# In layer two's expert loop, the preceding block's down products go in front of the last quarter of the up products, and the addition to the tokens goes behind it

## What is computed

```
out = 0
for e in range(16):
    g_, u_ = split(t @ w_gu[e])                        # w_gu[e] is 1024 x 1024
    out += gates[:, e] * ((silu(g_) * u_) @ w_dn[e])   # w_dn[e] is 512 x 1024
h = layer_norm(alpha * h + g2 * out)
```

## Time and profile before

| | |
|---|---|
| time, median of 3 runs | 1627.43 us (1623.88 to 1629.74) |
| profiled execution: its own time | 1631.9 us |
| profiled execution: its span, first to last instruction | 1630.1 us |
| PE busy over the span | 1527.2 us (94%) |
| DVE, ACT, POOL busy over the span | 871.2, 371.1, 271.4 us (53%, 23%, 17%) |
| mean granted TensorE clock | 0.979 of full speed |
| HBM read | 356.66 MB |

### The profile page before, as it was taken

How to read it: one execution, slowest core, us unless ns; L and a number is a source line. 1 busy time by engine, 2 the same in 40 slices (tenths; PEclk the granted TensorE clock), 3 DMA queues, 4 the chain that set the end, 5 groups by cost and what they waited for, 6 DMA issues and landing times.

```text
span 1630.1 us, 31680 instructions
## 1 busy us (share of the span) xinstructions
PE 1527.2 (94%) x13300; PEld 973.5 (60%) x13300; DVE 871.2 (53%) x1553; ACT 371.1 (23%) x893; POOL 271.4 (17%) x303
## 2 busy tenths in 40 slices
PE   6999999899999999898999886999999998999984
PEld 3454576564444468665666455757688887565642
DVE  3159946576777743652336437494552126554445
ACT  1100047541000010422222122003651002121211
POOL 0300000101112300042334230000000001543321
PEclk9999999999999999999999997999999999999998
DMA  9633220105857961999669968443125467999993
GB/s 319 195 104 94 78 68 27 51 28 182 274 154 247 326 222 63 357 414 385 240 261 407 414 271 303 145 120 98 48 61 189 143 220 285 396 415 415 414 416 115
DMA packets 147455, 365.23 MB, mean 224 GB/s; under 512 B 11265, under 2 KB 90729, under 8 KB 130419
## 3 DMA queue, kind: packets, MB, share of 16 engines
q1 hardware_dynamic: 125536, 296.86, 49.0%
q0 software_dynamic: 19328, 60.62, 11.1%
q10 hardware_dynamic: 2451, 5.73, 1.1%
HBM read 356.66 MB, written 10.62 MB: 225 GB/s over the span
## 4 chain that ended last, share of the span: by engine, by line
PE 66%; DVE 5%; DMA 5%; ACT 2%; SPq 1%; issue 1%; DVEq 0%; ACTq 0%; POOLq 0%
PE psum L1166 64%; DMA yab<-in_moe_w_gu 3%; DMA arena<-in_moe_w_gu 1%; PE psum L1703 1%; SPq L931 1%; DVE ring L2772 1%; PE psum L1450 0%; DMA convT<-us,x_row 0%; DVE st L2197 0%; DVE H L2794 0%; DMA yab<-ys 0%; DVE st L2198 0%; PE psum L1272 0%; DVE H L2210 0%; ACT uT L1870 0%
## 5 line engine op out<-in xcount | busy, mean ns | idle before, releaser
L1166 PE MATMUL psum<-uT,ring 128*128 128x512 f32 (+1 forms) x1440 | 494.7, 501 | 5.1 <-ACT uT L1870 2.1
L1166 PEld LDWEIGHTS psum<-uT,ring 128*128 128x128 f32 x1440 | 272.9, 191 | 215.1 <-issue 196.8
L1166 PE MATMUL psum<-ring,mo_tok 128*32 128x256 f32 x4992 | 313.0, 385 | 21.9 <-DVE ring L2772 21.7
L1166 PEld LDWEIGHTS psum<-ring,mo_tok 128*32 128x32 f32 x4992 | 157.4, 111 | 127.2 <-DVE ring L2772 28.5
L1166 PE MATMUL psum<-ring,v_tok 128*32 128x256 f32 x2496 | 152.1, 385 | 0.5 <-ACT v_tok L2119 0.5
L2350 DVE SCALAR_TENSOR_TENSOR convT<-upad_extra,cwT,convT 128x512 f32<-128x512 f32 (+1 forms) x240 | 132.4, 614 | 2.1
L1166 PEld LDWEIGHTS psum<-ring,v_tok 128*32 128x32 f32 x2496 | 82.4, 112 | 56.3 <-issue 3.8
L1166 PE MATMUL psum<-ring,uT 128*128 128x256 f32 (+1 forms) x576 | 113.1, 357 | 0.0
L1166 PEld LDWEIGHTS psum<-ring,uT 128*128 128x128 f32 x576 | 99.3, 190 | 15.5 <-issue 4.2
L1166 PE MATMUL psum<-yab,ring 128*128 128x512 f32 (+1 forms) x256 | 85.2, 486 | 0.0
L1166 PE MATMUL psum<-qkT_mqk 32*128 32x256 f32 (+5 forms) x752 | 81.3, 410 | 2.8 <-DVE qkT_mqk L2733 0.9
(11 more groups left out here) (364 smaller groups left out, 1633.0 us busy)
## 6 DMA issues: line engine op xcount, KB each, us to landing
ring<-in_w_in SPq DMA_DIRECT2D x104, 512.0 KB, 4.8
uT<-in_moe_w_gu SPq DMA_DIRECT2D x22, 1024.0 KB
yab<-in_moe_w_gu SPq DMA_DIRECT2D x21, 1024.0 KB
arena<-in_moe_w_gu SPq DMA_DIRECT2D x21, 1024.0 KB
ring<-in_w_mod SPq DMA_DIRECT2D x32, 512.0 KB, 9.7
mv_tok<-in_w_mod POOLq DMA_DIRECT2D x32, 512.0 KB, 5.2
convT<-in_w_mod POOLq DMA_DIRECT2D x32, 512.0 KB, 5.6
qkT_mqk<-in_moe_w_gu SPq DMA_DIRECT2D x14, 1024.0 KB, 16.4
```

The source lines that it names most:

```text
L1166: return nc.tensor.matmul(dst, lhsT, rhs, start=start, stop=stop)
```

## The change

In the second layer only, `down(b - 1)` moves from the end of iteration b to the place behind `up(b, (4, 5))`, and `add_to_tokens(b - 2)` moves from there behind `up(b, (6, 7))`, to the end of the iteration. The first layer's order stays.

```diff
                     if b < nb:
                         up(b, (4, 5), loads)
+                    if l and b:
+                        down(b - 1, loads_before)
+                    if b < nb:
                         for p, i in quad_halves(l, b):
                             quad_transposes(p, i)
+                        up(b, (6, 7), loads)
                     if l and b >= 2:
                         add_to_tokens(b - 2)
-                    if b < nb:
-                        up(b, (6, 7), loads)
-                    if b:
+                    if l == 0 and b:
                         down(b - 1, loads_before)
```

## The result

| | before | after |
|---|---|---|
| median of the runs, us | 1628.59 (1623.88 to 1629.74, 4 runs) | 1646.52 (1645.72 to 1648.4, 4 runs) |
| ratio, with its 95% interval | | 1.0118 (1.0094 to 1.0142) |
| profiled execution, own time, us | 1631.9 | 1648.4 (span 1646.6) |

The change makes the kernel slower by 1.2%, some 18 us by the medians. The forecast was 42.3 us. The sign, the place and the engine that TensorE now waits for came out as forecast; the size is the second rival's, not the first's.

What follows compares the result with a forecast made beforehand. TensorE was taken to bound the stretch of experts with several blocks; 25.3 + 6 + 1.5 + 8 + 1.5 = 42.3 us on the median 1627.4 gave 1669 us, 2.6% slower. Range 1643 to 1684, likeliest 1660 to 1682.

Steps and rivals of the forecast that it cites:

- rival 2: GpSimd slips in between two copies: eleven iterations lose 1.2 us each, total 15, with clock drops 20; 1642 to 1648; chance 0.26.
- the first's: The forecast itself: both waits, half clock in none to all of eleven iterations; 1660 to 1679, or 1682; chance 0.57.
- U + 0.28: GpSimd's matrix, held by the late addition, starts 0.28 us after an iteration's start U and ends at U + 1.50.
- Down's cover by pair 2: Pair 2 alone covers down's wait for ScalarE's hidden-row copy; no loss taken, 3 us as upper bound.
- The releaser named by the chain: At the loop's end the chain of waits names a transfer landing at 1593.66; the prediction called that misleading.
- One shuts out the other for whole instructions: VectorE copies and GpSimd instructions block each other fully; GpSimd gets nothing done between two copies in a row.
- eleven iterations under two copies: Iterations 3 to 25 where a new expert's copies start: hidden rows end behind both copies, 2.3 us lost each, 25.3 us.
- twelve others: Remaining iterations from 3 to 25: transposes wait for hidden rows behind the late matrix, 0.5 us each, 6 us.
- eleven iterations with quad transposes: Quad transposes move by the same steps and cost the same, so no loss.
- the end, from iteration 26: Iteration 26 to the last addition: down's gain is lost again to GpSimd; 53.05 us against 51.6, 1.5 us more.
- half clock: Stalls of 2.3 us may halve TensorE's clock: 8 us for the eleven, 1.5 us for the single-block stretch.

Runs made afterwards that it cites:

- the halved transfers: Kernel before, with the last two experts' weight transfers cut to half their bytes: 1625.9 us, ratio 0.9998; the same cut with a third matrix buffer in the new order: 1618.83 us.
- the third buffer: Kernel after, with room for three matrices, so block b's matrix waits for the addition of block b-3: 1625.68 us, ratio 0.9997 to before.
- down alone: Against the kernel before, only down moves forward, and the addition stays ahead of pair 3's products: 1629.04 us, ratio 1.0021.
- the addition alone: Against the kernel before, only the addition moves to the iteration's end; down keeps its place behind pair 3: 1666.75 us, ratio 1.0247.
- one-input hidden rows: Kernel after, with layer two's hidden rows made by a TENSOR_SCALAR, silu factor left out: 1669.76 us, ratio 1.0256 to before.

## Why the prediction was right in kind and wrong in size

**Right.** TensorE bounds the stretch, so a wait there costs its full length. The matrix stands behind the late addition and starts at U + 0.28 (measured 0.28). GpSimd's hidden rows are the releaser in eleven long and twelve short waits. The sign that the prediction gave for rival 2, eleven stalls near 1.2 us, is the one that came. Down's cover by pair 2 holds (one wait for ScalarE, 0.40 us, at the very end). The releaser named by the chain is misleading: shown by the halved transfers.

**The step that failed** is, in the prediction's words, "One shuts out the other for whole instructions, and GpSimd got nothing done between two copies in a row", carried from the matrix to the hidden rows. The rows it rested on are of the matrix, a one-input instruction; the hidden rows have two inputs, and these take their turn at the end of the first copy: 1.23 us lost in each of eleven iterations and not 2.3. The sentence "no row of before has hidden rows under two copies" is true of the second layer only. The first layer's loop of the same kernel makes its hidden rows by the same instruction, and six times it stands under two copies back to back:

```profile
710.52 1.12 POOL L1084 TENSOR_TENSOR qkT_mqk<-qkT_mqk 128x128 f32<-128x128 f32 x1 [1.35 <-ACT qkT_mqk L2126]
```

```profile
710.11 1.21 DVE L2772 COPY ring<-qkT_mqk 128x2048 f32<-128x2048 f32 x1
711.24 1.48 DVE L2772 COPY ring<-upad_extra 128x2048 f32<-128x2048 f32 x1
```

These hidden rows end at 711.64, 0.32 us behind the first copy, and the second copy is stretched, as in the kernel after. So the profile of before already spoke for rival 2, which was given 0.26. Term by term:

| term | forecast, us | measured, us |
|---|---|---|
| eleven iterations under two copies | 2.3 each, 25.3 | 1.23 each, 13.5 |
| twelve others | 0.5 each, 6 | 0.25 each, 3.0 |
| eleven iterations with quad transposes | 0 | some 0.13 each, 1.4 |
| the end, from iteration 26 | +1.5 | 0 |
| half clock | 8 + 1.5 | 0 |
| the start of the loop | 0 | -1.5 |

- The eleven: 1.23 against rival 2's 1.2.
- The twelve: the hidden rows start 1.19 us behind the matrix (1409.23, 1410.42), not 1.38. In the kernel before the spacing was 1.38 also where no copy stood near, since there the hidden rows waited for ScalarE's silu at the end of it (matrix at 1413.52, row below). With the late matrix the silu is done by then (the row of 1410.42 has no wait). It was taken for part of the undisturbed spacing.

```profile
1414.90 0.46 POOL L1084 TENSOR_TENSOR qkT_mqk<-qkT_mqk 128x128 f32<-128x128 f32 x1 [0.16 <-ACT qkT_mqk L2126]
```

- The quads: iterations with quad transposes take 8.55 and 7.60 us where one took 7.20 before; 8.55 - 7.20 - 1.23 and 7.60 - 7.20 - 0.25 leave 0.12 and 0.15. The kernel with the third buffer has no wait there and shows the same 0.14, so it belongs to the order. The quad transposes stood in front of the addition, and now products of up follow them; with down alone, where the addition still follows them, they cost nothing extra. That an extra change of tile form is the cause is argued, not shown.
- The end: the rounds took 8.17, 10.62, 10.14, 9.16 and 6.87 us (forecast 8.05, 10.8, 10.8, 9.85 and 7.1). Here the matrix really was held up (4.25, 4.50 and 4.50 us), so this part, built on the same rule, was nearly right. The end of before holds two stretches at half clock and that of after none, so the equal 51.6 us are in part the clock's.
- The clock: no half-clock stretch from 1364 to 1633.7. The forecast for it hung on the stall of 2.3 us. Where stalls did reach 2.2 us, in two of the experiments, four of nine and four of eleven were followed by half clock; a probability of one in two had been taken.
- The start: down(0) now fills part of a wait for the gathered tokens. The forecast had looked at iterations 3 and later only. As said above, the 1.5 us may be of these two executions alone; by the medians the loss is 17.9 us, all of it in iterations 3 to 25.
- The DMA engines were forecast to fall below 400 GB/s in the stretch; they kept 413.

Rival 2's sum, 13 + 6 - 4 = 15, is close in part by luck: of its three terms only the first was right. The twelve cost half of its 6, the end gave none of its 4, and the quads' 1.4 stood in no rival.

The measured terms from iteration 3 on give 13.5 + 3.0 + 1.4 = 17.9. Two small things outside the table cancel in that sum: one more matrix met a copy (1.54 us, 0.3 lost), and two quad iterations that took 7.40 and 7.43 us before have lost their extra 0.2 each.

The Trainium skill ("SBUF — State Buffer", the single rule under "Who interferes with whom") says that only the shared port pair causes contention and that it is an exclusive lock. The trace agrees where one instruction meets one copy: the matrix of 1440.09 in the kernel after, under a copy that ends at 1440.54, ends 1.09 us behind it and takes 1.54 in place of 1.22, a wait and not a slower rate. It does not fit the matrix that takes 2.40 us with the addition alone: 0.55 us without a copy and 0.25 us behind the next one are all that it had, so its 1.22 us were not one piece, and a whole copy passed in between. The prediction named 1.2 us as what the rule would give if GpSimd could take the pair between two copies, and then preferred the one contrary row. Both were true, of two forms of instruction.

## What to carry to other kernels

A late wait in an in-order queue costs what stands behind it: either swap the two instructions (here one line, the hidden rows ahead of the matrix) or give the waiting one another buffer, before judging the reorder that caused it. When the price of a stall is taken from a row of another kind of instruction, look through the whole trace, other layers too, for a row of the right kind; where there is none, both ends of the bound deserve nearly the same chance, and one kernel that swaps the kind settles it. And a reorder that shortens a round at the end of a stream of weights is worth only what the last transfers leave, even if they are no bound today.

## What the runs showed of the hardware

- **Who gets its turn behind the first of two copies depended on GpSimd's form.** Under back-to-back VectorE copies of 128 x 2048 (1.22 us each), a GpSimd TENSOR_TENSOR that had met the first copy was done 0.3 to 0.5 us behind its end: 1.42 us for 128 x 128 and 1.47 for 128 x 256, and the next copy stretched to 1.47 and 1.57. A TENSOR_SCALAR in the same place was passed over by the second copy, which kept its 1.21 to 1.23: 2.62 us for 128 x 128, 3.10 for 128 x 256. Seen with both roles swapped. Why was not tried.
- **It is no rule for every boundary.** Under four copies in a row the matrix, a TENSOR_SCALAR, took 4.25 us, or 4.50 with the last copy stretched to 1.42 and its own end 0.25 us behind that. With the addition alone it was done 0.25 us behind a copy although the next followed back to back, stretched to 1.41, and a whole copy had passed between the two parts of its work (2.40 us). What decides there is open.
- **On GpSimd the form with two inputs is the faster one here.** Alone, 128 x 256 in fp32: TENSOR_TENSOR 0.61 us, the TENSOR_SCALAR with two operations and per-partition scalars 1.22 us. For 128 x 128 with one operation: 0.46 against 0.61 us. How much of the 1.22 is the second operation was not separated.
- **Idle times of 2.2 us were followed by half clock in some cases only:** 4 of 9 with the addition alone and 4 of 11 with one-input hidden rows, all in iterations 3 to 25. None of those near 1 us was, nor the three of 2.54, 2.07 and 2.06 at the end of the kernel after.
